# Where the pooling mixer stands beside w_down, and which engine adds up its norms

## The reference, cut to what matters

```python
for i in range(DEPTH):                       # 4
    h = rmsnorm(x, norm_mix[i])
    if i % 2 == 0: y, v  = gmlp_mixer(h, ...)   # u, v = gelu(h @ w_in); v = rmsnorm(v, g_v)
                                                # y = (u * (mask(w_s) @ v + b_s)) @ w_out, chunks of 128
    else:          y, pb = pool_mixer(h, ...)   # (mean of the last 2/4/8/16 rows - h) @ w_pool * scale
    x = x + y                                   # pb: the last 15 normed rows
    h = rmsnorm(x, norm_ffn[i])
    y, cb = conv_ffn(h, ...)                    # (silu(conv3(h @ w_gate)) * (h @ w_val)) @ w_down
    x = x + y
return rmsnorm(x, norm_final), ...              # rmsnorm: x * rsqrt(mean(x*x) + eps) * gain
```

## Time and profile before

| | |
|---|---|
| Time, median of 6 runs | 2827.84 us |
| Profiled execution | 2850.1 us, span of its slowest core (core 7) 2848.6 us |
| Spans of the eight cores | 2808.2 to 2848.6 us |
| PE busy, core 7 | 2767.3 us, 97% of the span, 18404 matmuls |
| DVE, ACT, POOL busy, core 7 | 1499.5 (53%), 1201.2 (42%), 466.3 us (16%) |
| Chain that ended last | PE 85%, DVE 4%, DMA 4%, issue 4%, ACT 2% |

### The profile page before, as it was taken

One profiled execution on the slowest core, in us unless ns is written; L12 is line 12 of the kernel. 1 busy time (PEld: TensorE's weight loads), 2 busy tenths in 40 slices (PEclk: granted clock), 3 DMA queues, 4 the chain that ended last, 5 costly groups with the idle time before them and its releaser, 6 DMA issues.

```text
span 2848.6 us, 52255 instructions; the slowest of 8 cores (2808.2 to 2848.6 us)
## 1 busy us (share of the span) xinstructions
PE 2767.3 (97%) x18404; PEld 1749.8 (61%) x18404; DVE 1499.5 (53%) x3160; ACT 1201.2 (42%) x2362; POOL 466.3 (16%) x827
## 2 busy tenths in 40 slices
PE   7999999999999999999989999999999999999998
PEld 3456666666655666666656566666666466666665
DVE  3466644764236564376433766447631656627633
ACT  4434434643343343464335344355424434435421
POOL 1011321223101132222210110110021020020000
PEclk9999999999999999999989999999999999999988
DMA  7653444353444344425274335244425453413611
GB/s 154 114 105 60 77 87 75 64 102 66 75 75 82 60 76 88 76 57 108 59 183 93 60 60 99 52 76 76 76 56 97 72 97 73 78 32 60 115 28 59
DMA packets 40591, 227.82 MB, mean 80 GB/s; under 512 B 6256, under 2 KB 6896, under 8 KB 23024
## 3 DMA queue, kind: packets, MB, share of 16 engines
q0 software_dynamic: 33200, 193.77, 38.6%
q1 hardware_dynamic: 7136, 30.72, 3.1%
HBM read 406.34 MB, written 13.32 MB: 147 GB/s over the span
## 4 chain that ended last, share of the span: by engine, by line
PE 85%; DVE 4%; DMA 4%; issue 4%; ACT 2%; DVEq 0%; ACTq 0%; SPq 0%; POOL 0%; POOLq 0%
PE psum L740 28%; PE psum L1021 22%; PE psum L1028 22%; PE psum L822 7%; PE psum L845 3%; DMA xT_47<-x_in 1%; DMA w_144<-wts 1%; PE psum L933 1%; DVE vn_68 L859 1%; DMA gmlp_v<-gout 1%; PE psum L669 1%; DVE vn_69 L859 1%; DVE nwt L766 0%; PE psum L984 0%; DVE nwt L767 0%
## 5 line engine op out<-in xcount | busy, mean ns | idle before, releaser
L1045 DVE SCALAR_TENSOR_TENSOR cb_130<-psum,pvf,cb_130 128x384 f32<-128x384 f32 (+1 forms) x264 | 150.8, 571 | 61.0 <-ACT cb_130 L1035 39.0
L1045 DVE SCALAR_TENSOR_TENSOR cb_128<-psum,pvf,cb_128 128x384 f32<-128x384 f32 (+1 forms) x264 | 150.9, 571 | 57.6 <-ACT cb_128 L1035 36.0
L1045 DVE SCALAR_TENSOR_TENSOR cb_127<-psum,pvf,cb_127 128x384 f32<-128x384 f32 (+1 forms) x264 | 150.9, 571 | 55.9 <-ACT cb_127 L1035 43.4
L1045 DVE SCALAR_TENSOR_TENSOR cb_129<-psum,pvf,cb_129 128x384 f32<-128x384 f32 (+1 forms) x264 | 150.7, 571 | 49.8 <-ACT cb_129 L1035 34.5
L1035 ACT ACTIVATE cb_130<-psum,pvf 128x384 f32<-128x384 f32 (+2 forms) x132 | 84.4, 640 | 100.7 <-PE psum L1021 99.5
L1035 ACT ACTIVATE cb_128<-psum,pvf 128x384 f32<-128x384 f32 (+2 forms) x132 | 84.4, 640 | 98.0 <-PE psum L1021 97.4
L1035 ACT ACTIVATE cb_127<-psum,pvf 128x384 f32<-128x384 f32 (+2 forms) x132 | 84.5, 640 | 96.3 <-PE psum L1021 95.9
L1035 ACT ACTIVATE cb_129<-psum,pvf 128x384 f32<-128x384 f32 (+2 forms) x132 | 84.6, 641 | 94.9 <-PE psum L1021 94.5
L854 DVE TENSOR_TENSOR vstat_114<-vstat_114 128x1 f32<-128x1 f32 (+1 forms) x18 | 2.8, 157 | 201.0 <-ACT junk L852 201.0
L1052 POOL TENSOR_SCALAR stmp_121<-ASb,pvf 128x64 f32<-128x64 f32 x88 | 38.8, 441 | 402.5 <-ACT ASb L1038 400.2
L1057 ACT ACTIVATE cb_129<-cb_129 128x384 f32<-128x384 f32 (+2 forms) x132 | 65.1, 493 | 71.5 <-DVE cb_129 L1045 62.2
(11 more groups left out here) (1233 smaller groups left out, 6721.6 us busy)
## 6 DMA issues: line engine op xcount, KB each, us to landing
ASb<-st_conv SPq DMA_DIRECT2D x4, 1056.0 KB, 7.4
gvb<-g_v SPq DMA_DIRECT2D x4, 1024.0 KB, 6.2
xT_43<-x_in SPq DMA_DIRECT2D x2, 768.0 KB, 7.2
xT_44<-x_in SPq DMA_DIRECT2D x2, 768.0 KB, 6.7
y_out<-yT_52 SPq DMA_DIRECT2D x2, 768.0 KB, 3.7
xT_46<-x_in SPq DMA_DIRECT2D x2, 768.0 KB, 6.5
y_out<-yT_55 SPq DMA_DIRECT2D x2, 768.0 KB, 16.3
xT_47<-x_in SPq DMA_DIRECT2D x2, 768.0 KB, 33.0
```

Of the source, the lines that this page charges most:

```text
L1045: rec(DVE, lambda e: e.scalar_tensor_tensor(out=cb.t[:, 0:npr], in0=pap(gb, 2 - sh, 2 - sh + npr), scalar=sc(3 * l + 2 - sh), in1=cb.t[:, ...
```

## The change

Seven edits, in the order of the diff:

1. The first tile of x comes in four parts; the first weight unit is queued behind the first of them.
2. `pool_stat` keeps only rcol. The samples' rows move into `pool_rows`: ACT evicts the sums, 14 operations of 64 columns on GpSimd do the Newton iteration, and two operations on GpSimd replace the 8 on DVE. In the second group GpSimd first copies the 15 rows, and `pool_rows` is called at the end of tile 2's mixer.
3. `proj_tile` gets a hook `mid` after block dc = 2. Through it the mixer of tile t-1 is recorded inside w_down of tile t.
4. The sums of squares behind the mixer of tiles 0 and 1 go by `stat_add` (ACT, GpSimd, DVE, one matmul), not by the array. Tile 2 keeps the array. L933 now also waits for rcol.
5. The Newton iteration is shorter: no shift, and for one column a fused step; with the sum of halves 9 operations in place of 13 for one column, 11 in place of 12 for two or three.
6. One transfer each for brow and browS; gout is written after both halves of vn.
7. `first_norm` of the second group's tiles 1 and 2 is recorded inside the first `mixer_a` of that group.

```diff
@@ load_x, start
+        def load_x(g, t, behind=(), parts=2):
+            w = KC // parts
+            for h in range(parts):
+                ks = slice(w * h, w * h + w)
-        xl0 = load_x(0, 0)
+        xl0 = load_x(0, 0, parts=4)
@@ pool_stat
-            if t != 2:
-                return
+            if t == 2 and g == 0:
+                pool_rows(g, t, l)
+            elif t == 2:
+                rec(POOL, lambda e: e.tensor_copy(out=hpp.t[:, :, :], in_=xv[(g, t)].t[:, :, 241:256]), ...)
+        def pool_rows(g, t, l):
             rec(PE, lambda e: e.matmul(pap(pr, 0, m), lhsT=meanb.t[:], rhs=ab.t[:, lo:lo + m], ...
-            rsqrt_dve(lambda: pap(pr, 0, m), rtail.t[:, 0:m], rtail.all, m, pt=[(pr, False)])
+            rec(ACT, lambda e: e.activation(out=t0, in_=pap(pr, 0, m), func=AF.Identity, bias=epsb.t[:, 0:1]), ...)
+            ptiny(lambda e: e.tensor_scalar(out=i2, in0=i0, scalar1=-0.5, scalar2=1597463007.0, ...))
+            ptiny(lambda e: e.tensor_scalar(out=t0, in0=t0, scalar1=-0.5, scalar2=None, op0=ALU.mult))
+            for k in range(3):
+                ptiny(lambda e: e.tensor_tensor(out=t1, in0=t2, in1=t2, op=ALU.mult))
+                ptiny(lambda e: e.tensor_tensor(out=t1, in0=t1, in1=t0, op=ALU.mult))
+                ptiny(lambda e: e.tensor_scalar(out=t1, in0=t1, scalar1=1.5, scalar2=None, op0=ALU.add))
+                ptiny(lambda e: e.tensor_tensor(out=dst_ap, in0=t1, in1=t2, op=ALU.mult), ...)
-            for kc in range(KC):
-                rec(DVE, lambda e: e.scalar_tensor_tensor(out=dst.t[:, kc, :], in0=xv[(g, t)].t[:, kc, lo:lo + m], ...
+            rec(POOL, lambda e: e.tensor_tensor(out=dst.t[:, :, :], in0=src, in1=gain, op=ALU.mult), ...)
+            rec(POOL, lambda e: e.tensor_tensor(out=dst.t[:, :, :], in0=dst.t[:, :, :], in1=rtail.t[:, 0:m].unsqueeze(1).to_broadcast([128, KC, m]), ...
@@ proj_tile
+                if mid is not None and dc == 2:
+                    mid()
@@ rsqrt_dve
-            tiny(lambda e: e.tensor_scalar(out=i1, in0=i0, scalar1=1, scalar2=None, op0=ALU.logical_shift_right))
-            tiny(lambda e: e.tensor_scalar(out=i2, in0=i1, scalar1=-1.0, scalar2=1597463007.0, ...))
+            tiny(lambda e: e.tensor_scalar(out=i2, in0=i0, scalar1=-0.5, scalar2=1597463007.0, ...))
+            if w == 1:
+                tiny(lambda e: e.tensor_scalar(out=t0, in0=t0, scalar1=-0.5, scalar2=None, op0=ALU.mult))
+                    tiny(lambda e: e.scalar_tensor_tensor(out=t1, in0=t2, scalar=t0, in1=t2, ...))
@@ mixer_a
-            for q in range(4):
-                dma(POOL, brow.t[32 * q:32 * q + 1, :], b_big[j, q:q + 1, :], ...)
+            dma(POOL, brow.t[0:128:32, :], b_big[j], ...)
+                if g > 0 and l == 0 and u == 2 and t < 2:
+                    first_norm(g, t + 1)
-                rec(DVE, lambda e: e.tensor_tensor(out=vs.t[0:nt, 2:3], in0=vs.t[0:nt, 0:1], in1=vs.t[0:nt, 1:2], op=ALU.add), ...)
-                for half in range(2):
+                for dst_b in (vb, gout)[0:2 if nt == NSM else 1]:
+                    for half in range(2):
@@ mixer_b_tile
+                        rec(PE, mmz, reads=wp.all + rcol[t].all + [hB.r[(kc, t)] ...
-                    stat_add_pe(g, t, ec)
-                stat_finish(g, t, pe=True)
+                    if t == 2:
+                        stat_add_pe(g, t, ec)
+                    else:
+                        stat_add(g, t, ec)
+                stat_finish(g, t, pe=(t == 2))
+                if g > 0 and t == 2:
+                    pool_rows(g, t, l)
@@ ffn, driver
-                proj_tile(g, t, mm_list, l + 1 if l % 2 == 0 else None, l == DEPTH - 1)
+                proj_tile(g, t, mm_list, l + 1 if l % 2 == 0 else None, l == DEPTH - 1,
+                          (lambda t=t: mixer_b_tile(g, l + 1, t - 1)) if l % 2 == 0 and t > 0 else None)
-                            if t > 0:
-                                mixer_b_tile(g, l + 1, t - 1)
```

More of the change, by code:

```diff
@@ L718, in pool_stat @@
                 reads=ab.all + meanb.all, pt=[(pr, True)], cost=0.1)
-            rsqrt_dve(lambda: pap(pr, 0, m), rtail.t[:, 0:m], rtail.all, m, pt=[(pr, False)])
-            dst = hS if g == 0 else hpp
-            for kc in range(KC):
-                rec(DVE, lambda e: e.scalar_tensor_tensor(out=dst.t[:, kc, :], in0=xv[(g, t)].t[:, kc, lo:lo + m],
-                                                           scalar=pvd.t[:, kc, l:l + 1], in1=rtail.t[:, 0:m], op0=ALU.mult, op1=ALU.mult),
-                    reads=[xv[(g, t)].r[kc]] + rtail.all + pvd.all, writes=dst.r.values(), cost=dvec(m, True))
+            t0, t1, t2 = (nwtail.t[:, i, 0:m] for i in range(3))
@@ new lines, in pool_rows, with ptiny @@
+            i0, i2 = (nwtail.t[:, i, 0:m].bitcast(I32) for i in (0, 2))
+            tr = nwtail.all
+            rec(ACT, lambda e: e.activation(out=t0, in_=pap(pr, 0, m), func=AF.Identity, bias=epsb.t[:, 0:1]), pt=[(pr, False)], reads=epsb.all, writes=tr, cost=actc(m, True, 1))
+            def ptiny(f, w_=tr):
+                rec(POOL, f, reads=tr, writes=w_, cost=poolc(m))
+            ptiny(lambda e: e.tensor_scalar(out=i2, in0=i0, scalar1=-0.5, scalar2=1597463007.0, op0=ALU.mult, op1=ALU.add))
@@ new lines, in pool_rows @@
+            dst = hS if g == 0 else hpp
+            gain = pvd.t[:, :, l:l + 1].to_broadcast([128, KC, m])
+            src = xv[(g, t)].t[:, :, lo:lo + m] if g == 0 else hpp.t[:, :, :]
+            rec(POOL, lambda e: e.tensor_tensor(out=dst.t[:, :, :], in0=src, in1=gain, op=ALU.mult),
+                reads=(xv[(g, t)].all if g == 0 else hpp.all) + pvd.all, writes=dst.all, cost=poolc(KC * m))
+            rec(POOL, lambda e: e.tensor_tensor(out=dst.t[:, :, :], in0=dst.t[:, :, :], in1=rtail.t[:, 0:m].unsqueeze(1).to_broadcast([128, KC, m]), op=ALU.mult),
+                reads=dst.all + rtail.all, writes=dst.all, cost=poolc(KC * m))
@@ L935, in mmz @@
                             return i
-                        rec(PE, mmz, reads=wp.all + [hB.r[(kc, t)] for kc in range(4 * zh, 4 * zh + 4)], pt=[(bk, True)], cost=mmc(4, 256))
+                        rec(PE, mmz, reads=wp.all + rcol[t].all + [hB.r[(kc, t)] for kc in range(4 * zh, 4 * zh + 4)], pt=[(bk, True)], cost=mmc(4, 256))
                         rec(ACT, lambda e: e.activation(out=zt.t[:, zh, :], in_=pap(bk), func=AF.Copy, scale=rcol[t].t[:, ci:ci + 1]),
```

65 lines of the change are left out of this document (33 added, 32 removed).

## The result

The changed kernel takes 2770.65 us in the median, 57 us less than before. The ratio is 0.9797, with a 95% interval from 0.9788 to 0.9806. "Before" beside an experiment is the kernel before on the same chip, 2827.4 to 2828.6 us.

A forecast was written before the change was run, and what follows sets the result against it. TensorE, busy for nearly all of the span, was taken to bound the kernel, with small, many waits. Savings of 43.7 less 4.0 gave 39.7: 2827.84 - 39.7 = 2788 us; own range 2780 to 2796, 8-in-10 range 2770 to 2808.

The forecast's parts named there:

- Sums off the array: TensorE's sums of squares behind the mixer: 56 fewer matmuls at 0.16 us each save 9.0 us.
- Mixer inside w_down: Four stretches where w_down meets the pooling mixer: 17.9 us without TensorE, of which 11.9 are saved.
- What is added: GpSimd's samples' rows and adds: L948 waits 1.0 us twice (-2.0); new waits for the adds cost another -2.0.
- Rival B: At L948: the pool_rows chain takes 14.7 us or longer, waits of 3.8 to 6 us twice; 2796 us, chance 0.12.
- Contention: Pooling stretches: new waits for GpSimd's adds, with DVE's operations lengthened, cost 0.5 us per stretch, -2.0; bounds 0 and -18.
- rival A: Pooling stretches: DVE and GpSimd slow each other, TensorE's stalls move into w_down; 2802 us, chance 0.22.
- Short chain: Newton chain on DVE: four fewer operations per chunk, the small waits for vn nearly vanish, saving 7.8 us.
- Bias rows: GpSimd's brow transfers: weights w_141 to w_144 start earlier and the 4.3 us wait for w_144 goes, saving 5.5 us.
- Large v waits: Two large waits for vn behind the v chunks, at gout's transfer: 1.4 us saved each, 2.8 in all.
- Start and switch: TensorE's start wait for w_137 shrinks by 1.7 us; waits at the switch of groups shrink by 2.5.
- Rival C: Pooling stretches, large v waits and switch: the gaps close more than forecast, 16 us further; 2772 us, chance 0.12.
- Rival D: GpSimd's weight transfers start late behind its added adds and TensorE waits in four layers; 2847 us, chance 0.04.

The follow-up runs named there:

- the five kernels: Changed kernel with mixer back behind the tile 2795.6 us, sums back on the array 2777.3; kernel before with sums alone 2839.9, place alone 2817.6, both 2808.7.

## Why the prediction was right, and where it was short

The forecast, faster, holds. 2770.65 lies inside the range of 2770 to 2808 by 0.65 us, less than the 5.7 us that a measurement of this kernel can tell, so that the range held is luck. The forecast itself, 2788, was 17 us too slow, and the time is outside its own range of 2780 to 2796. The five edits that were undone one at a time cost 25.1, 6.9, 14.3, 10.1 and 7.7 us, 64 in all where the whole change gave 57: they overlap, and the prices can't be added. By the steps:

- *Sums off the array, 9.0.* Right: TensorE's weight loads, one for each matmul, fall from 18404 to 18348 as forecast, and its work by 8.9 on core 0 in the run with this edit alone. That alone it makes the kernel slower was not in the prediction: I took the new way of the sums for hidden, and it is, but only in the mixer's new place. That the array needs the place, and the place the sums, is shown by the five kernels.
- *Mixer inside w_down, 11.9.* The number came out by help of another step. The idle time of the stretches fell from 17.8 to 3.8 on core 0, by 14.0. But with place and sums alone it fell to 13.4, by 4.4 only, and with all but the rows' edit it was 11.8. Most of the 14.0 needs the samples' rows off VectorE as well.
- *What is added, -2.0 for the samples' rows.* This term was wrong, in sign and size. I priced the 14 small operations as a load on GpSimd and left out what 20 operations fewer free on VectorE. Undone, the edit costs 10.1. My reading of L933's waits as ScalarE being late was not at fault: in the kernel before, rcol_119 is written 11.9 us or more ahead of z_77 in all four stretches, and ScalarE had other work in between. On core 3, VectorE and ScalarE:

```profile
496.95 0.15 DVE L771 SCALAR_TENSOR_TENSOR rcol_119<-nwt 128x2 f32<-128x2 f32 x1
```

```profile
509.58 1.50 ACT L937 ACTIVATE z_77<-psum,rcol_119 128x512 bf16<-128x512 f32 x2
```

Rival B is out: the chain takes 8.9 us on GpSimd (from 495.35 to 504.23) and 9.4 with ScalarE's eviction, which starts at 494.87, where I had worked out 8.9 with it; and L978 never waits.

```profile
495.35 0.25 POOL L734 TENSOR_SCALAR nwtail<-nwtail 128x64 int32<-128x64 int32 x1 [5.31 <-ACT nwtail L730]
...
502.00 1.27 POOL L747 TENSOR_TENSOR hS<-hS,rtail 128x512 f32<-128x512 f32 x1
...
503.42 0.81 POOL L750 CAST hPS<-hS 128x512 bf16<-128x512 f32 x1
```

- *Contention, -2.0.* It is there. Eight operations that write hB took 4.33 us in layer 1 before (core 3); in the changed kernel (core 0), where two to three of GpSimd's adds fall into them, they take 5.62:

```profile
506.74 4.33 DVE L692 SCALAR_TENSOR_TENSOR hB<-xT_44,pvd,rstd_99 128x384 bf16<-128x384 f32 x8 [0.65 <-ACT rstd_99 L684]
```

```profile
487.49 5.62 DVE L693 SCALAR_TENSOR_TENSOR hB<-xT_44,pvd,rstd_99 128x384 bf16<-128x384 f32 x8 [0.65 <-ACT rstd_99 L685]
```

On core 0 of both kernels such a group of eight takes 4.32 or 4.33 us with no add beside it and 4.93 to 5.07 beside one whole add; beside eight of `pool_rows`' operations over 15 columns (at 2540.03) it takes 4.33. The rule of the Trainium skill (SBUF — State Buffer, section "SBUF: two separate sides") would hold VectorE for the whole of an add, about 1 us each; the loss here is about 0.75 us for an add (5.07 less 4.32), so the trace agrees that VectorE loses time, though less than that. On TensorE little of it arrives: L710, which stands behind such a group, waits 0.8 us for VectorE in all, and the four stretches have 3.8 us of idle. So rival A is out for this kernel.

- *Short chain, 7.8, and clock.* Undone it costs 14.3 where the terms for it and the large waits were 10.6. I counted a wait at its row. Across the kernel the clock gave back 8.3 us on core 0, where I had 2.5 and about 1 in the bias term, and TensorE's work fell by 13.5 where the columns are 8.9. What the other 4.6 are stays open. That each stop also costs work is not shown: with the long chain 8.9 us more idle came with 2.6 more work, but with the mixer behind the tile 15.5 more idle came with 0.8.
- *Bias rows, 5.5:* 7.7 when undone; core 1 of that run has 4.0 us more idle than core 0 of the changed kernel and 2.5 more lost to the clock. *Large v waits, 2.8:* on core 0 they were 3.57 and 4.21 before and are 2.90 and 2.21 now, 2.7 less, as forecast; the run without gout's overlap took out 8 us.
- *Start and switch, 4.2:* not undone. On core 0 the first u product starts at 14.68 in place of 16.64, but the wait for w_138 behind it grew from 4.5 to 5.9, and that product starts at 32.95 in place of 33.05: nothing is left of the 1.7. The switch hardly moved (6.0 and 6.1 on core 0 now, 6.1 and 7.4 before).
- *Rival C* has the number (2772) but not the way: the pooling stretches closed further, while the v waits and the switch gained no more than my terms. *Rival D:* no wait for a weight unit appears at the pooling layers.

## What to carry to other kernels

An operation moved to an idle engine is priced on both engines: the queue that it leaves may be the one that holds up the chain. The operation that a wait names is the one that ended last, not always the one that was needed (rtail above, where a PSUM bank was): look in the kernel for what the waiting operation reads and writes. Two edits that each look like a saving can be worth nothing alone, since one makes the time that the other needs; and a scheduler that is told another cost or size changes the order of all streams, so a run with one edit undone compares two orders as well.

## What the runs showed that I had not expected

TensorE's short stops came with a lower clock: in the long-chain run 8.9 us more idle with 2.0 us more lost to the clock, with the mixer behind the tile 15.5 with 8.9. Neighbouring cores of a pair end about 12 us apart in the changed kernel, and a transfer that is late on one (5.9 us for weights of v with six bias loads) was not on the other. VectorE's operations on hB were lengthened by GpSimd's adds of 384 or 320 columns and not by its operations of 15 columns; those took 0.34 to 0.55 us beside VectorE's group at 2540.03 and 0.21 to 0.26 right behind it. GpSimd's product of 128x512 took 1.06 us at 482.11 and 1.27 at 502.00, no longer than the 1.35 worked out from 128x384.
